# Two more one-time places for expert weights, and single 1 MB pieces loaded along the recurrence, in a fused two-block transformer kernel

## The reference, cut to what matters

```
xn    = rms_norm_2(h, norm1_gain)
proj  = xn @ w_in
ret   = silu(...) * head_norm(retention(q, k, v))            # 4 heads of 128
rw    = rwkv7_time_mix(proj[..., 2048:], ...)                # 8 heads of 64, a recurrence over the tokens
h     = h + concat([ret, rw]) @ w_out
xn    = rms_norm_2(h, norm2_gain)
# 32 experts in 4 groups; each token goes to the best 2 experts of its best group
for each expert e with its tokens x_e:
    y_e = (silu(x_e @ w_gate[e]) * (x_e @ w_up[e])) @ w_down[e]    # 1024 x 512, 1024 x 512, 512 x 1024
h     = h + sum over the two experts of weight * y_e
out   = rms_norm_2(h, final_norm_gain)
```

## Time and profile before

| what | value |
|---|---|
| median of 3 runs (lowest to highest) | 1046.9 us (1046.47 to 1047.34) |
| profiled execution, its own time | 1047.48 us |
| its span in the trace | 1045.7 us |
| mean granted clock of TensorE | 0.973 |
| PE busy | 900.0 us (86%) |
| DVE busy, ACT busy | 436.9 us (42%), 318.1 us (30%) |
| read from DRAM | 290.77 MB |
| chain that ended last | PE 55%, DMA 31%, SP's queue 5%, DVE 5% |

### The profile page before, as it was taken

How to read it: one execution, slowest core, us unless ns; L and a number is a source line. 1 busy time by engine, 2 the same in 40 slices (tenths; PEclk the granted TensorE clock), 3 DMA queues, 4 the chain that set the end, 5 groups by cost and what they waited for, 6 DMA issues and landing times.

```text
span 1045.7 us, 17915 instructions
## 1 busy us (share of the span) xinstructions
PE 900.0 (86%) x7768; PEld 642.5 (61%) x7768; DVE 436.9 (42%) x553; ACT 318.1 (30%) x410; POOL 17.5 (2%) x34
## 2 busy tenths in 40 slices
PE   5999999999999998999999997776868677677854
PEld 5999988999999878999988732221313122121311
DVE  4577777666656437996676510000101010010101
ACT  4457674554444327644443400000000000000002
POOL 1300000000000000000000000000000000000000
PEclk9999999999999999999999999998989888998999
DMA  9994334555654544353019999999999999999994
GB/s 338 269 325 147 133 111 162 161 162 171 204 190 161 201 155 163 129 205 115 3 56 387 420 398 422 422 421 420 421 421 423 421 422 422 421 422 423 422 421 193
DMA packets 84439, 294.97 MB, mean 282 GB/s; under 512 B 5903, under 2 KB 35231, under 8 KB 59664
## 3 DMA queue, kind: packets, MB, share of 16 engines
q1 hardware_dynamic: 79280, 284.18, 69.8%
q10 hardware_dynamic: 3552, 6.08, 1.6%
q0 software_dynamic: 1536, 3.68, 1.3%
HBM read 290.77 MB, written 4.10 MB: 282 GB/s over the span
## 4 chain that ended last, share of the span: by engine, by line
PE 55%; DMA 31%; SPq 5%; DVE 5%; issue 2%; ACT 1%; DVEq 0%; ACTq 0%
PE psum L986 13%; DMA arena<-in_w_down 13%; PE psum L987 13%; PE psum L988 13%; DMA arena<-in_w_up 12%; DMA arena<-in_w_gate 5%; SPq L837 5%; PE psum L1572 4%; PE psum L1315 3%; PE psum L961 2%; PE psum L1592 2%; DVE ring_rounded L2055 1%; PE psum L953 1%; PE psum L1061 1%; DVE arena L2103 1%
## 5 line engine op out<-in xcount | busy, mean ns | idle before, releaser
L1572 PE MATMUL psum<-arena,featL 128*32 128x512 f32 x1024 | 172.1, 657 | 63.6 <-DMA arena<-in_w_up 48.6
L2055 DVE TENSOR_TENSOR ring_rounded<-arena,hi_rounded 128x2048 fp32r<-128x2048 f32 x77 | 176.0, 2290 | 94.7 <-ACT hi_rounded L1677 93.8
L1677 ACT ACTIVATE hi_rounded<-arena 128x2048 fp32r<-128x2048 f32 x77 | 146.7, 1912 | 157.5 <-PE psum L988 52.4
L986 PE MATMUL psum<-hi_rounded,featT_rounded 128*128 128x256 f32 (+1 forms) x560 | 165.2, 295 | 4.7 <-DVE featL_rounded L2071 3.9
L987 PE MATMUL psum<-ring_rounded,featT_rounded 128*128 128x256 f32 (+1 forms) x560 | 162.6, 290 | 0.0
L988 PE MATMUL psum<-hi_rounded,featL_rounded 128*128 128x256 f32 (+1 forms) x560 | 162.5, 290 | 0.0
L1572 PEld LDWEIGHTS psum<-arena,featL 128*32 128x32 f32 x1024 | 38.7, 118 | 184.9 <-DMA arena<-in_w_up 86.3
L1592 PE MATMUL psum<-arena,featT 128*32 128x512 f32 x488 | 91.7, 673 | 40.9 <-DMA arena<-in_w_down 36.0
L986 PEld LDWEIGHTS psum<-hi_rounded,featT_rounded 128*128 128x128 f32 x560 | 108.0, 193 | 8.3 <-DVE ring_rounded L2055 4.2
L987 PEld LDWEIGHTS psum<-ring_rounded,featT_rounded 128*128 128x128 f32 x560 | 108.1, 193 | 1.2
L988 PEld LDWEIGHTS psum<-hi_rounded,featL_rounded 128*128 128x128 f32 x560 | 108.0, 193 | 1.3
(11 more groups left out here) (295 smaller groups left out, 1138.9 us busy)
## 6 DMA issues: line engine op xcount, KB each, us to landing
arena<-in_w_gate SPq DMA_DIRECT2D x75, 1024.0 KB, 26.2
arena<-in_w_up SPq DMA_DIRECT2D x75, 1024.0 KB, 26.4
arena<-in_w_down SPq DMA_DIRECT2D x62, 1024.0 KB, 26.9
arena<-in_w_in SPq DMA_DIRECT2D x14, 2048.0 KB, 8.9
arena<-in_w_down SPq DMA_DIRECT2D x5, 2048.0 KB, 7.7
arena<-in_w_out SPq DMA_DIRECT2D x3, 2048.0 KB, 8.6
arena<-in_w_in SPq DMA_DIRECT2D x4, 1024.0 KB, 9.6
t_copies<-arena ACTq DMA_DIRECT2D x1, 2048.0 KB, 8.0
```

The source lines that it names most:

```text
L986: mm(o, lhs[0], rhs[0], start=start, stop=False, skip_group_check=True)
L1572: ins = mm(psum[32 * j:32 * j + 32, MB[4 + m], :], xg[:, 4 * half + k, 32 * j:32 * j + 32], quad[place(q, j)][j][:, 512 * k:512 * k + 512] ...
L1677: fn(high, view, ACT.Copy).then_inc(hi_ready, 1)
L2055: tt(low, view, high.bitcast(F32), ALU.subtract).then_inc(lo_ready, 1)
```

## The change

- **Two more places.** For the pieces j = 2 and j = 3 of quad 1 there is a place NQ + 2, split over memory that is dead by then: for j = 2 half of `featL` and two parts of `featT`, for j = 3 the 1024 columns of `rows` that later hold `final_gain`, a part of `featT`, and a new tensor `late`. Their 1 MB are loaded by 2 and by 3 DMAs. 23 pieces can now be issued before PE has read any. `FIRST[j]` gives the places of the first quads for each j.
- **Single pieces early.** SP issues a piece as soon as its own memory is free: 8 pieces between the retention output and the last U (before: 6, and all from `mixed_ready` = 2 on). For that, some tensors are moved: S to the recurrence's half of `xn`, P2T to slot 11 of M, the mask `mle` to another part of `cst`.
- **Order on the engines.** PE runs `state_keys(0)` ahead of the WT matmuls; ACT makes the square root for `ret_scale(1)` ahead of the copies of Q and gn; DVE runs `ret_scale(1)` ahead of the additions of step TT.
- **`final_gain`** is loaded when `pieces_read` reaches 8 (its memory is a place until then), after POOL's four products of the router, where before it was loaded when the logits were filled.

```diff
-        RELEASED = ((("U", NCH - 1, 1), ((0, 0),)), (("Y", 1, 1), ((1, 0), (1, 1), (1, 2), (1, 3))))
-        ONCE = (2, 1, 1, 1)
+        ONCE = (2, 1, 2, 2)
+        FIRST = [(*PLACES, NQ, NQ + 1)] * 2 + [(PLACES[0], NQ + 2, *PLACES[1:], NQ)] * 2
...
+        SPLIT = {2: (featL[:, 4:8, :].rearrange("p a b -> p (a b)"), spent[:, LE["sg"][0]:LE["h"][1]]),
+                 3: (final_gain, spent[:, LE["GT"][0]:LE["gap"][1]], late[:])}
...
                     elif once(r, pair, q - NQ, j):
-                        sp.wait_ge(pieces_read, 4 * (q - NQ - ONCE[j]) + (j + 1))
+                        sp.wait_ge(pieces_read, 4 * FIRST[j].index(quad_place(r, pair, q, j)) + (j + 1))
...
+                    wait_filled(sp, "ro", NT - 1)
+                    place_free(2, 0)
+                    wait_filled(sp, "inv", "X1", NT - 1)
+                    place_free(2, 1)
+                    wait_emptied(sp, "mat", "Aak", 1)
+                    place_free(NQ, 0)
+                    wait_filled(sp, "mat", "Arb", 1)
+                    place_free(3, 3)
+                    sp.wait_ge(mixed_ready, 1)
+                    place_free(2, 2)
+                    wait_filled(sp, "gn", NT - 1)
+                    place_free(NQ, 1)
+                    wait_filled(sp, "mat", "Ark", 1)
+                    place_free(3, 2)
                     sp.wait_ge(mixed_ready, NT)
-                    load_quad(0, 0, 0, pieces=(1, 2, 3))
-                    wait_emptied(sp, "mat", "Ark", 1)
-                    load_quad(0, 0, NQ, pieces=(0, 1))
-                    for key, pieces in RELEASED:
-                        wait_filled(sp, *key)
-                        for q, k in pieces:
-                            load_quad(0, 0, q, pieces=(k,))
+                    wait_filled(sp, "U", NCH - 1, 1)
+                    place_free(2, 3)
+                    wait_filled(sp, "Y", 1, 1)
+                    place_free(3, 0, 1)
                     sp.wait_ge(mixed_ready, 2 * NT)
-                    load_quad(0, 0, NQ, pieces=(2,))
-                    load_quad(0, 0, 2, pieces=(2,))
+                    place_free(NQ, 2)
+                    place_free(1, 2)
                     wait_filled(sp, "wo2", 0, 1)
-                    load_quad(0, 0, 2, pieces=range(2))
-                    load_quad(0, 0, 3, pieces=(3,))
+                    place_free(1, 0, 1)
+                    place_free(0, 3)
                     wait_filled(sp, "wo2", 1, 0)
-                    load_quad(0, 0, 2, pieces=(3,))
-                    load_quad(0, 0, 3, pieces=(0,))
+                    place_free(1, 3)
+                    place_free(0, 0)
                     wait_filled(sp, "wo2", 1, 1)
-                    load_quad(0, 0, 3, pieces=(1, 2))
+                    place_free(NQ + 2, 2, 3)
+                    place_free(0, 1, 2)
                     wait_filled(sp, "logit", NT - 1)
-                    load_quad(0, 0, NQ, pieces=(3,))
+                    place_free(NQ, 3)
                     sp.wait_ge(xn_ready, 2 * NT)
                     sp.wait_ge(scattered, 2 * NT)
-                    load_quad(0, 0, NQ + 1, pieces=(0,))
-                    load_quad(0, 0, NQ + 1, pieces=(1, 2, 3))
-                    for q in range(NQ + 2, 12):
+                    place_free(NQ + 1, 0)
+                    load_quad(0, 0, NQ + 1, pieces=(1,))
+                    load_quad(0, 0, NQ + 2, 8, pieces=(0, 2, 3, 1))
+                    for q in range(NQ + 3, 12):
                         load_quad(0, 0, q, 4 * (q - NQ))
...
-            wait_filled(pool, "logit", NT - 1)
-            nc.gpsimd.dma_start(final_gain, A["final_gain"].to_broadcast([P, D])).then_inc(gain_in, 16)
...
+            pool.wait_ge(pieces_read, 8)
+            nc.gpsimd.dma_start(final_gain, A["final_gain"].to_broadcast([P, D])).then_inc(gain_in, 16)
```

73 lines of the change are left out of this document (43 added, 30 removed).

## The result

The changed kernel takes 1050.83 us (median of 10 runs, 1048.41 to 1053.24), the kernel before 1046.35 in the same measurement. The ratio is 1.0039, with a 95% interval of 1.0022 to 1.0056: slower, where 1042.7 was forecast and 1046.2 was the end of the range. The profiled execution has 1049.60 us and a span of 1047.8, against 1047.48 and 1045.7.

The account below looks back on a forecast made before the run. From about 604 us full DMA engines bound the kernel, a count of pieces to come. Gains of 3.2 (stream), 0.46 (`state_keys(0)`) and 0.5 (instruction supply) made 4.2 us, from the 1046.9 median to 1042.7, range 1040.4 to 1046.2.

Parts of the forecast that it names:

- All three signs of "wrong": First expert matmuls after 597.8; new issue stalls over 0.5 us at 499 to 545; DMA rate below 400 at 588, 598 or 603.
- Instruction supply: PE in the recurrence: 1.6 us of the 2.05 stall at 557 goes, five flights add some 1.1; gain 0.5 us.
- rival C: Recurrence: single pieces starve PE's instruction supply, five flights each with a 2.05 us stall, 8.2 us longer; 1051.4 us, chance 0.08.
- Places and order of issue: Expert weight stream: 0.7 of a piece more landed by 576.11 and the gap at 601 closed; gain 3.2 us.
- margin of 0.0 us at 588.6: Projection's trigger at 586.84 plus 1.73 us restart was to meet the ring's end at 588.6 just in time.
- rival B: Stream from 574 on: the ring misses its turns, or small DMAs and lone pieces cost 1.73 us restarts; middle 1045.2, chance 0.17.
- I cost them at nothing: Split place's two pieces as five DMAs of 256 to 512 KB: no cost, as 421 GB/s holds across queued DMAs.
- Final gain: final_gain's 512 KB load now falls into the full ring and costs 1.25 us, counted within the 3.2.
- `state_keys(0)` and `ret_scale(1)`: Recurrence: state_keys(0) fills PE's 0.94 us wait ahead of WT, gain 0.46; ret_scale(1) fits DVE's idle 3.15 us, costs nothing.
- The early pieces: Ahead of the projection: only 12 pieces of room, so almost nothing of the 54 idle us before 543.9 is usable.
- D: SP's order: an early wait comes late, fewer than 12 pieces landed at 574.38; 1046.4 to 1048 us, chance 0.06.

Follow-up runs that it names:

- e1: Changed kernel, but SP waits for mixed_ready = 2 ahead of the first expert piece, so none is in flight before about 539 us; 1047.88 us, 0.9998 of before.
- e5: Changed kernel with the piece issued when gn is filled moved behind the wait for Ark (about 551 us); 1045.41 us, 0.9967 of before.
- e2: Changed kernel without the split place: 21 places, final gain loaded at the logits, early pieces and orders kept; 1050.49 us, 1.0026 of before.
- e4: e1 with six additional, unread 1 MB loads at the changed kernel's early triggers; 1053.82 us, 1.0052 of before.
- e9: The changed kernel itself, timed again beside e10 on one chip; 1050.04 us, 1.0010 of before.
- e17: e8 with one extra 1 MB load issued when gn is filled, no other flight before the first pieces; 1046.63 us, 0.9986 of before.
- e3: Kernel before with only the new engine order: state_keys(0), ret_scale(1) and ACT's square root where the change puts them; 1049.01 us, 1.0015 of before.
- e7: e8 with only the j = 2 piece split, in two DMAs, and final_gain at the logits; 1046.94 us, 0.9990 of before.
- e8: Changed kernel with waits for mixed_ready's last and the first U ahead of the first piece; 1046.41 us, 0.9987 of before.
- e10: Changed kernel with the piece issued at gn moved to when WT is filled, about 5 us later; 1046.38 us, 0.9979 of before.
- e11: e5 with the split place's five DMAs issued behind place 0's two pieces; 1046.29 us, 0.9979 of before.
- e12: e5 with only j = 2 of the split place, behind place 0's pieces, and final_gain issued at mixed_ready's last; 1045.93 us, 0.9974 of before.
- e13: e12 with gn's piece behind WT and not behind Ark; 1048.62 us, 1.0010 of before.
- e18: e10 repeated on another chip; 1048.99 us, 1.0005 of before.
- e14: Kernel before with only final_gain moved behind the eighth piece read; 1049.01 us, 1.0013 of before.
- e6: Kernel before with the new places and late final_gain alone, order and first triggers as before; 1047.28 us, 0.9994 of before.
- e15: Kernel before with only the last two pieces freed at 586.84 us issued as five DMAs into the old places; 1047.13 us, 0.9998 of before.
- e16: e6 with one extra 1 MB load issued when gn is filled; 1046.57 us, 0.9988 of before.

## Why the prediction was wrong

The median is 8.1 us above the forecast. By the traces' marks the recurrence was forecast 0.96 shorter (0.46 and 0.5) and came 3.5 longer, the stream was forecast 3.2 shorter and came 0.3 longer, and 0.4 were added between them: 8.4. All three signs of "wrong" came: the first expert matmuls at 599.55, stops of 0.58, 0.82 and 0.55 ahead of 543 and 0.89 at 543.79, and 304 GB/s at 590 to 597.

*Instruction supply: the step that failed.* It stood in the sum as a gain of 0.5 us. `ro` to the last Y became 3.5 us longer, or 3.9 with the 0.4 that `state_keys(0)` gained. I had counted short stops of 0.22 at five flights. There were some (0.58, 0.49, 0.82, 0.55, 0.30), about as in e1, and one of 2.23. The mechanism was rival C's, with its chance of 0.08, but not its count: one flight, behind the others, did it and not five. C's time, 1051.4, came near by luck: it had 8.2 us more in the recurrence and a stream that gains 3.2. What no term had was the clock behind the stop. e5, without the stop, is 3.5 us shorter from L1389 to the last Y though it has a stop of 0.73 there that the changed kernel lacks, which makes 4.2. The stop itself delays PE's next matmuls by 0.85 (the chain's 0.89 less the 0.04 that e5 has); the rest, some 3.3, is put down to the clock: that is also half of the 6.51 us for which PE was busy from 546 to 553.

That the flight at 537.83 is a condition is shown: the low clock at 546 to 556 stands in the four traces with five flights and then one at `gn` (changed, e2, e4, e9) and in none of the other 16. That earlier flights are a second condition follows from e17. Which of them was not tried alone, but the block packets point at the double issue at 531. Behind it no block moves for 6.3 to 7.0 us in all ten traces that have it (529.56 to 536.46 in the changed kernel); in the other ten, the blocks between 520 and 539 begin 3.4 to 4.6 us apart. When the block that PE needs behind the WT matmuls begins to move, counted from the start of these matmuls:

| kernels with the new order on PE | begin of the block, us | PE idle behind the WT matmuls |
|---|---|---|
| no piece in flight ahead of 536 (e1, e3, e7, e8, e17) | -3.9 to -3.4 | for ACT's copies only |
| early pieces with the double issue, none at `gn` (e5, e10, e11, e12, e13, e18) | -1.3, e11 -0.8 | the same, or stops of 0.3 (e12) and 0.6 (e11) |
| the same and the flight at `gn` (changed, e2, e4, e9) | +0.7 to +1.5 | 1.9 to 2.7 |

So the double issue uses up PE's lead of 3.4 us or more down to about 1.3, and the flight at `gn` takes 2 us or more beyond it. In the changed kernel, e2, e4, e9 and e17 the block begins 0 to 0.5 us ahead of the end of that load's data, so it stands behind them. What isn't shown is whether one flight at 531 would be enough, and why the block waits for nearly the whole load and not for a part of it.

The Trainium skill ("Runtime: NRT & Kernel Launch", "Instruction fetch mechanics") calls the crossing of a block mostly hidden. These traces agree with the block's length (256 records, 16 KB) and not with the rest: the 113 stops in the recurrence cost 0.2 to 2.9 us each, and those where no piece was in flight up to 1.4 (e7, at 517.62).

*Places and order of issue: the term was mis-sized.* Forecast -3.2, measured +0.3 (F to the last down matmuls). What the term said of the gap was right: 601 to 604 is at 418 GB/s. Adding up the rates microsecond by microsecond, all but the last 1.05 MB have landed 428.6 us behind F before and 427.2 after: 1.4 us gained and not 3.2. The missing 1.8 is the stretch from 590 to 597, (421 - 304) / 421 x 7 = 1.95 us. There the margin of 0.0 us at 588.6 didn't hold: the trigger came at 588.55, the rate fell to 180 GB/s from 590 to 591, and the five DMAs that came first ran at 274 to 360 up to 596. This was rival B, costed at one restart of 1.73. Then the last megabyte took 6.0 us to PE's last matmuls and 4.3 before. The DMA rate there, in GB/s for each microsecond, from 1026 on before, from 1026.5 on after:

```
before  401 393 270 156   0   0
after   393 377 221 107  57  16
```

The stream runs out less evenly, which costs 1.7. In the four traces without the small DMAs (before, e2, e3, e14) this last part is 4.2 to 4.3 us; in the sixteen with them it is 4.9 to 6.0, but 4.0 in e17. "I cost them at nothing" was wrong therefore, at the stream's end alone by 0.6 to 1.7 us in 15 of 16 traces. Why, and why e17 is spared, is open. The Trainium skill ("DMA: Bandwidth & Descriptors", "Rules for kernel authors") asks for 1 MiB and more per DMA for the most bandwidth. The 304 and 310 GB/s of the changed kernel and e10 agree with it, e6's 403 behind a queue much less; the cost at the end of the stream it doesn't name.

*Final gain.* 1.25 was taken and 1.45 measured in e14's trace: right, as far as one trace and a ratio of 1.0013 (from 0.9997) can tell.

*`state_keys(0)` and `ret_scale(1)`.* Right where they stand (0.94 became 0.52, DVE still waits), but e3 shows that the gain doesn't reach the end: the triggers come earlier and the flood of pieces meets other ends of blocks.

*The early pieces.* As forecast they fill 12 places and no more, and the ring is dry from 575 to 578 (107 GB/s). They could bring little, and each was a risk to PE.

*D* is excluded: 12 pieces had landed, 12.8 MB by 576.1. Between the last Y and F the changed kernel has 0.4 us more than before. So have e2, e9, e10, e11, e13 and e18 (e7 has 0.6), and e5 hasn't. In these but e7 and e11 the chain has a stop of 0.57 us on DVE there (at 563.80 in the changed kernel), with nothing to wait for; its cause is open.

## What to carry to other kernels

Before filling an idle ring with early loads, count what they can bring (here 0.7 of a piece) and look at what the ring's silence was good for: PE's instructions wait behind the same loads, and a stretch of small matmuls uses up a block of them in about 4 us. Look at when the blocks move (the trace has their packets) and how far ahead of PE they are: two loads one behind the other took 2 us and more of that lead, and one more load was enough to stop PE. Cost a stop of 2 us once with its own length and once with the clock behind it. A margin of zero in a queue counts as a restart. What a piece in small DMAs costs at the end of the stream belongs into the sum too.

## What was not expected of the hardware

- All 113 stops "for nothing" of the recurrence end 1.2 to 1.6 us behind the landing of a block of instructions, whose packet can stand behind a load of 1 MB for most of its length.
- A stop of about 2 us costs its own length or, with the clock, some 3.3 us more. In the recurrence the clock was at 1.2 GHz for 3 to 8 us behind idle times of PE of 1.66 (e11) to 2.87 us (e15), and stayed at 2.4 behind 1.78 (e1), 2.05 (before, e16), 2.32 (e8) and 2.51 (e3).
- One DMA of 1 MB, issued 5 us earlier or later, made 3.7 us between two medians on one chip (e9, e10) and 4.6 us in the recurrence of their traces. In the repeat e18 the trace came out the same and the time did not (1.0005). And the same load without the others ahead of it cost nothing (e17).
- Five DMAs of 0.25 to 0.5 MB ran at 403 GB/s behind a queue and at 310 without one (e6, e10), and with them the stream's end was 0.6 to 1.7 us longer in 15 of 16 traces.
- In 11 of 20 traces the clock is at 1.2 GHz when the last down matmuls begin, and from there to the end it takes 16.1 to 17.7 us and not 14.7 to 15.5. That is as much as most of the effects looked for here.
